# The first norm's weights as one row, spread by TensorE, and a weight piece's lower half in two parts

## The reference, cut to what matters

```python
def rms_norm(x, g):
    xf = x.astype(jnp.float32)
    y = xf * lax.rsqrt(jnp.mean(xf * xf, axis=-1, keepdims=True) + EPS)
    return (y * g.astype(jnp.float32)).astype(x.dtype)
...
        hn = rms_norm(h, mix_pre_g)
        proj = hn @ w_in
...
        u = proj[..., D_Q + 2 * D_KV:]
...
    a, gate = jnp.split(u, 2, axis=-1)
    h = a * jax.nn.sigmoid(gate)
```

## Time and profile before

| | us |
|---|---|
| median of 3 runs | 2321.12 |
| lowest and highest | 2320.91, 2321.96 |
| the profiled execution, its own time | 2321.9 |
| its span in the trace | 2320.1 |
| TensorE busy | 2287.2 (99%) |
| VectorE busy | 1411.6 (61%) |
| ScalarE busy | 978.1 (42%) |
| GpSimd busy | 869.7 (37%) |

### The profile page before, as it was taken

One profiled execution on the slowest core, in us unless ns is written; L12 is line 12 of the kernel. 1 busy time (PEld: TensorE's weight loads), 2 busy tenths in 40 slices (PEclk: granted clock), 3 DMA queues, 4 the chain that ended last, 5 costly groups with the idle time before them and its releaser, 6 DMA issues. The chain is left out here.

```text
span 2320.1 us, 30750 instructions
## 1 busy us (share of the span) xinstructions
PE 2287.2 (99%) x11636; PEld 1920.8 (83%) x11636; DVE 1411.6 (61%) x2164; ACT 978.1 (42%) x1992; POOL 869.7 (37%) x749
## 2 busy tenths in 40 slices
PE   9999999999999999999999999999999999999998
PEld 8788888888888888888898878888888888888887
DVE  7999824955454577776533766153594545447776
ACT  4126634532323344456634755134453323234543
POOL 2000225388787800023112022121338878770003
PEclk9999999999999999999999999999999999999999
DMA  5222124233233368665002001243223323336855
GB/s 159 53 64 75 54 89 136 85 119 116 89 118 105 118 231 277 214 226 136 27 10 71 19 6 46 64 163 119 96 60 118 119 86 118 105 127 245 286 210 197
DMA packets 219589, 275.85 MB, mean 119 GB/s; under 512 B 17259, under 2 KB 144972, under 8 KB 216626
## 3 DMA queue, kind: packets, MB, share of 16 engines
q1 hardware_dynamic: 200594, 210.31, 29.2%
q10 hardware_dynamic: 18848, 63.58, 7.0%
HBM read 205.27 MB, written 68.57 MB: 118 GB/s over the span
## 5 line engine op out<-in xcount | busy, mean ns | idle before, releaser
L496 PE MATMUL P<-ah,wh 128*128 128x512 f32 (+1 forms) x1136 | 441.3, 388 | 0.2 <-DVE al L526 0.2
L498 PE MATMUL P<-ah,wl 128*128 128x512 f32 (+1 forms) x1136 | 438.9, 386 | 0.0
L497 PE MATMUL P<-al,wh 128*128 128x512 f32 (+1 forms) x1136 | 438.6, 386 | 0.0
L496 PE MATMUL P<-wh,ah 128*128 128x512 f32 (+2 forms) x1128 | 426.0, 378 | 0.0
L498 PE MATMUL P<-wh,al 128*128 128x512 f32 (+2 forms) x1128 | 423.3, 375 | 0.0
L497 PE MATMUL P<-wl,ah 128*128 128x512 f32 (+2 forms) x1128 | 422.9, 375 | 0.0
L578 POOL TENSOR_TENSOR stats<-stats,epsc 128x1 f32<-128x1 f32 x78 | 32.9, 422 | 762.4 <-ACT xn L1892 422.3
L496 PEld LDWEIGHTS P<-ah,wh 128*128 128x128 f32 x1136 | 213.4, 188 | 43.7 <-issue 0.7
L498 PEld LDWEIGHTS P<-ah,wl 128*128 128x128 f32 x1136 | 213.4, 188 | 43.4
L497 PEld LDWEIGHTS P<-al,wh 128*128 128x128 f32 x1136 | 213.5, 188 | 42.2
L498 PEld LDWEIGHTS P<-wh,al 128*128 128x128 f32 x1128 | 212.2, 188 | 36.9
(11 more groups left out here) (372 smaller groups left out, 4261.8 us busy)
## 6 DMA issues: line engine op xcount, KB each, us to landing
rf<-ff_rows SPq DMA_DIRECT2D x154, 256.0 KB, 5.2
stage<-in_w_down_dram SPq DMA_DIRECT2D x110, 256.0 KB, 3.9
ff_rows<-sb ACTq DMA_DIRECT2D x22, 1024.0 KB, 5.0
stage<-in_w_gu_dram SPq DMA_DIRECT2D x44, 512.0 KB, 5.2
stage<-in_w_in_dram SPq DMA_DIRECT2D x22, 512.0 KB, 3.9
stage<-in_w_gate_dram SPq DMA_DIRECT2D x22, 512.0 KB, 4.0
stage<-in_w_up_dram SPq DMA_DIRECT2D x22, 512.0 KB, 5.1
ff_rows<-uo ACTq DMA_DIRECT2D x22, 512.0 KB, 3.0
```

The source lines that it names most:

```text
L496: e.matmul(out, lh, rh, start=start, stop=False, skip_group_check=onto)
L497: e.matmul(out, lh, rl, start=False, stop=False, skip_group_check=onto)
L498: return e.matmul(out, ll, rh, start=False, stop=stop, skip_group_check=onto)
```

## The change

The load of the first norm's weights becomes one row of 4 KB into partition 0 of `GB[1]`, the first x tile is issued ahead of it and of the unit matrix. A row of ones is set in `causal` by VectorE. TensorE, ahead of its fillers, multiplies the ones (1 x 128, stationary) with the row (1 x 512, moving) twice, into banks 4 and 5, and VectorE copies the two banks to `GB[1]`, ahead of its first norm; the norms wait for the copies. GpSimd makes the lower half of weight piece 0 in two parts of 512 columns with a signal each, and the first quarter waits for the first part before its first step and for the second before its fifth.

```diff
@@ input_loads
+        row(0)
+        e.dma_start(GB[1][0:1, :], I["mix_pre_g"].rearrange("(a n) -> a n", a=1)).then_inc(*l_gb[1].up("x"))
         e.dma_start(ident[:, :], I["c_ident"]).then_inc(*l_const.up("ident"))
-        row(0)
-        e.dma_start(GB[1][:, :], I["mix_pre_g"].partition_broadcast(128)).then_inc(*l_gb[1].up("x"))
         row(1)
@@ x_norm
-        DV.wait_ge(l_gb[1], "x")
+        for i in range(2):
+            DV.wait_ge(ev, ("gx", i))
@@ u_quarter
-            PE.wait_ge(*lows(c))
+            PE.wait_ge(*((wl, ("half", 0)) if i == 0 else lows(c)))
...
         for k in range(8):
+            if k == 4 and half == 0:
+                PE.wait_ge(*lows(c))
@@ new functions
+    def gain_rows_pe():
+
+        PE.wait_ge(zf, "ones_row")
+        PE.wait_ge(l_gb[1], "x")
+        for i in range(2):
+            claim(4 + i, ev, ("gx", i))
+            PE.e.matmul(P[:, 4 + i, :], causal[0:1, :], GB[1][0:1, 512 * i:512 * i + 512], start=True, stop=True).then_inc(
+                *mm.up(("gx", i)))
+
+    def gain_rows_dve():
+        for i in range(2):
+            DV.wait_ge(mm, ("gx", i))
+            DV.e.tensor_copy(GB[1][:, 512 * i:512 * i + 512], P[:, 4 + i, :]).then_inc(*ev.up(("gx", i)))
@@ mixer1_pe
         e = PE.e
+        gain_rows_pe()
         turn_unit_matrix(16)
@@ mixer1_dve
+        e.memset(causal[0:1, :], 1.0).then_inc(*zf.up("ones_row"))
...
+        gain_rows_dve()
         x_norm(0)
@@ mixer1_pool
+    def first_low():
+
+        PL.wait_ge(wh, 0)
+        for key, cs in ((("half", 0), slice(0, 512)), (0, slice(512, 1024))):
+            PL.e.tensor_tensor(WL[0][:, cs], stage[place(0)][:, cs], WH[0][:, cs].bitcast(F32), ALU.subtract).then_inc(
+                *wl.up(key))
+        lowered[0] = 1
...
-        low_to(0)
+        first_low()
```

## The result

The changed kernel takes 2325.02 us (median of 20 runs, 2323.05 to 2326.32), the kernel before 2321.40 (20 runs, 2320.83 to 2323.13): ratio 1.0014, with an interval of 1.0008 to 1.0020. In a second measurement it was 2325.24 against 2321.07 (1.0017, 1.0009 to 1.0026). So it is slower by about 3.6 us (4.2 in the second), and the forecast, 2321.3 in a range up to 2324.0, was too low.

What follows compares the result with a forecast made beforehand. TensorE, busy 2287.2 of 2320.1 us, was taken as the bound. The start's terms summed to +0.2 us, so 2322.1 for the profiled execution and, 0.8 lower for the median, 2321.3 us; range 2319.3 to 2324.0.

Steps and rivals of the forecast that it cites:

- (1): Loads at the start: tile 0 lands at about 4.7 us, the gain's row at 4.5, tile 1 near 6.8.
- (2): TensorE's two added one-row products: 1.8 us each, from 4.5 to 8.1 us.
- (3): VectorE's two copies out of PSUM, 0.69 us each: tile 0's norm starts at about 8.9, not 7.24.
- (5): GpSimd's lower half in two parts: the first is there at 14.9 us, taking back 0.5 us.
- (4): TensorE from 8.1 us: clock rises in the middle of the 16 fillers; first product at about 15.45, as before.
- (6): Chain to the second quarter, before at 21.04 us: mostly absorbed in a wait, +0.2 us in all.
- rival (a): TensorE's clock rises late, only after tile 1's turn starts: +1.7 us, 2322.9; chance 15%.
- the base: Whole-kernel time: profiled execution 2321.9 us, median 0.8 lower at 2321.12; the same difference applied to the changed kernel.
- What moves the second moves the end by as much: Start of the second quarter, 21.04 us: any shift there shifts the kernel's end equally.
- rival (b): TensorE's clock does not rise before the first quarter is over: +6.3 us, 2327.5; chance 4%.

Runs made afterwards that it cites:

- before_again: The kernel before run once more with nothing edited, a single run: 2321.14 us.
- split_only: The kernel before with only the lower half of weight piece 0 made in two parts: 2321.41 us against 2321.07, ratio 1.0003.
- padded: The kernel before with three more VectorE memsets and 18 TensorE fillers in place of 16 at the start: 2322.56 us.
- padded_dve: The kernel before with three more VectorE memsets at the start and nothing else: 2321.80 us.
- padded_pe: The kernel before with 18 TensorE fillers in place of 16 and nothing else: 2321.15 us.
- after_plus_two: The changed kernel with two more VectorE memsets of 32 elements at the start: 2324.56 us.

## Why the prediction was wrong

Parts (1), (2), (3) and (5) held, each but for the times that part (4) pushed back. Loads: 4.26, 4.5 and 7.17 for 4.7, 4.5 and 6.8. Products: 3.67 us for 3.6. First norm: 9.16 for 8.9, released by the copy. The split: its first part was there by 15.9, ahead of the rows, where the whole would have ended at about 17.0 (14.60 and 2.36, an estimate) and held the first product up by 0.5; alone it was worth nothing. Part (6) held as well: from the first product to the second quarter it is 5.66 us after and 5.58 before, and 5.42 to 5.68 in the other three traces.

**The step that failed is (4), "I let it rise in the middle of the 16 fillers".** TensorE's work was unbroken from 4.5, but the one-row products did not help to raise the clock: the same products over 128 rows bring the rise at 8.70, over one row it came at 12.03, 14.44, 14.38 and 13.36. So the fillers take 3.67 and not 2.7 us and part or all of tile 0 is slow too. The second quarter is at 22.14 to 23.01, not 21.2; the first trace alone is 0.94 off, within the 1 us that the prediction allowed, but there the time moved all the same. This was rival (a), which I gave 15% and 2322.9. Its mechanism came true, its time was 2.1 us too low. What it named as speaking for it, that the fillers of the earlier trace rows did not bring the rise, decided nothing, and its real argument, that a one-row product may not count, had no price of its own.

**The second failing step is the base**, "with the same difference gives 2321.3". The profiled execution of before was one with the late clock (rise 13.90), 0.8 us above the median of three; its start is 0.72 behind that of before_again, which took 0.76 less. The changed kernel had the late rise in all four traces, so that nothing was to be subtracted. The fillers of the earlier trace rows were taken not to bring the rise because they had not in that one trace; in others they did.

By the rule of the Trainium skill, "TensorE: Matmul & The Clock Gate" (What's actually happening), that the moment of the rise differs from run to run of one kernel, the traces agree: 5.71 and 13.90 for the kernel before, 12.03 to 14.44 for the changed one. It should have moved the base of the sum and not only rival (a).

**A premise that failed** is "What moves the second moves the end by as much": in the first trace the second quarter moved by 1.10 us and the end by 3.39. The memset and the copies were to "cost nothing" beyond their own time; three more instructions on VectorE cost 0.3 us a thousand microseconds later, which no row of before could have given.

In rival (b), which did not come, 24 products at twice 0.12 us are 2.9 us more, not 2.2.

**The sum as the traces give it.** Second quarter, changed: mean of 22.14, 23.01, 22.97 and 22.83, 22.74. With the start of before: mean of 21.04, 20.32, 20.15, 20.19, 20.50 and 21.02 (before, before_again, split_only, padded, padded_dve, padded_pe), 20.54. So 2.2 us: 1.7 of it against the 21.04 of the earlier trace rows, where parts (4) and (6) had 0.2 together, and 0.5 from the base. The two waits less what is gained back ahead of them, 0.3. At the very end the changed kernel lost another 0.75, 0.33, 0.16 and 0 us, mean 0.3, where ScalarE waits for stores. Together 2.8 of 3.6, where the interval of the ratio is 1.9 to 4.6 us. The fall near 200 us is in two of four traces of the changed kernel and in three of those six, so it is not put down to the change; whether it is more frequent there stays open, and with it the last 0.8 us.

## What to carry to other kernels

Fillers that are to bring TensorE's clock up should be full-height work: here two products with one row in them kept the engine busy for 3.7 us and did not bring the rise, and the same products over 128 rows did. Fillers that reached from one piece of work nearly to the next kept the risen clock, but in this kernel that gained no time that could be measured. Before a few microseconds of the start are costed from one trace, find out whether its clock rose early or late, since the same program has both. When three instructions more or less move a kernel of two milliseconds by 0.3 us, a gain of that size has to be read from the traces at the place of the change, not from the total.

## What the runs showed that I had not expected

The rise depends on how many rows a product has: two float32 products of 1.8 us each, alike in start, columns and duration, brought it at 8.70 with 128 rows (127 of them zeros; one trace) and not before 11.30 with one (after_plus_two; 12.03 to 14.44 in the changed kernel's four traces). A risen clock can fall again at the start when TensorE idles for 2.2 to 2.5 us (at 9.13, 9.33, 10.41 and 11.27 in four kernels), but need not: in split_only it idled for 2.23 us and the clock stayed up. Three VectorE memsets of 0.1 us at 1 us bring waits of 0.24 and 0.28 us at 1135 and 1358, of which 0.2 is gained back elsewhere. And with the first two loads exchanged the third landed at 8.98 in place of 7.05, in one trace, though the bytes ahead of it were the same.
